# Front of a hybrid layer reordered: early modulation block, five weight buffers, moments of one tile first; GpSimd makes the filter parts' differences and VectorE their sums

## What is computed

```python
sh1, sc1, g1, sh2, sc2, g2 = split(silu(c) @ w_mod + b_mod, 6)   # once for c_ctx, once for c
u = layer_norm(x) * (1.0 + sc1) + sh1
q, k, v, xr, gate, hy = split(u @ w_in)
# hyena filters, for L = 128 and L = 512:
h = sin(freq[0] * (feats @ w1 + b1))
h = sin(freq[1] * (h @ w2 + b2))
h = (h @ w3).reshape(L, 4, 256) * exp(-t * abs(decay))
# forward and backward parts make one circular filter, used through its Fourier transform
filt_f = rfft(concat([f_fwd, 0, flip(f_bwd[:, 1:])]))
```

## Time and profile before

| what | value |
|---|---|
| median of three runs | 634.93 us (634.59, 634.93, 637.37) |
| the profiled execution's own time | 633.17 us |
| its span | 631.3 us |
| TensorE busy | 600.8 us, 95% |
| VectorE busy | 440.5 us, 70% |
| ScalarE busy | 305.6 us, 48% |
| GpSimd busy | 188.4 us, 30% |
| mean granted clock of TensorE | 0.997 |

### The profile page before, as it was taken

The page is one execution under the profiler, slowest core; times in us unless marked ns, Lnnn a source line. Parts: engine busy times, 40 slices in busy tenths (PEclk is TensorE's granted clock), DMA queues, the critical chain, the costliest instruction groups (busy, mean ns, idle before and its releaser), DMA issues.

```text
span 631.3 us, 9327 instructions
## 1 busy us (share of the span) xinstructions
PE 600.8 (95%) x3353; PEld 455.3 (72%) x3353; DVE 440.5 (70%) x757; ACT 305.6 (48%) x506; POOL 188.4 (30%) x152
## 2 busy tenths in 40 slices
PE   6899999999999988998999999989999999999994
PEld 2237999999999965557888888747767677676352
DVE  4967766834994654467553499988998877983187
ACT  2748122335344543005795342846565655752354
POOL 1002333345551307041496070421212221321121
PEclk9999999999999999999999999999999999999998
DMA  9985852222221269764980706769999999999788
GB/s 305 387 305 222 305 186 97 101 101 100 101 68 66 92 238 325 303 264 99 290 271 36 294 8 234 280 168 370 393 376 403 390 388 406 374 364 372 291 299 144
DMA packets 40040, 154.89 MB, mean 245 GB/s; under 512 B 7049, under 2 KB 17033, under 8 KB 27451
## 3 DMA queue, kind: packets, MB, share of 16 engines
q1 hardware_dynamic: 27912, 115.41, 50.6%
q10 hardware_dynamic: 5522, 23.48, 9.4%
q0 software_dynamic: 6560, 15.42, 8.3%
HBM read 141.59 MB, written 23.63 MB: 262 GB/s over the span
## 4 chain that ended last, share of the span: by engine, by line
PE 82%; DVE 7%; DMA 5%; ACT 4%; issue 2%; POOL 0%; DVEq 0%; ACTq 0%; POOLq 0%
PE bank L1898 13%; PE bank L1574 12%; PE bank L1575 12%; PE bank L1770 9%; PE bank L1952 8%; PE bank L1410 3%; PE bank L1747 2%; PE bank L1674 2%; PE bank L1880 2%; DMA arena<-in_w_mod 2%; PE bank L1477 2%; PE bank L1625 2%; PE bank L2011 2%; PE bank L1730 2%; DMA u_scr<-arena 1%
## 5 line engine op out<-in xcount | busy, mean ns | idle before, releaser
L772 POOL TENSOR_TENSOR w_low<-arena,w_high 128x1024 fp32r<-128x1024 f32 x22 | 53.6, 2437 | 145.9 <-ACT w_high L971 145.9
L2544 DVE TENSOR_TENSOR gate_up_low<-arena,gate_up_high 128x1024 fp32r<-128x1024 f32 x64 | 75.3, 1221 | 12.3 <-ACT gate_up_high L1256 10.2
L1256 ACT ACTIVATE gate_up_high<-arena 128x1024 fp32r<-128x1024 f32 x64 | 63.9, 1054 | 15.5 <-DMA arena<-in_moe_w_gu 15.5
L971 ACT ACTIVATE w_high<-arena 128x1024 fp32r<-128x1024 f32 x22 | 23.2, 1058 | 87.8 <-PE bank L1575 87.0
L1574 PE MATMUL bank<-u_high,w_high 128*128 128x320 f32 x176 | 56.3, 320 | 1.7 <-DVE u_low L2157 1.7
L1952 PE MATMUL bank<-arena 128*128 128x512 f32 x128 | 57.7, 593 | 0.0
L1575 PE MATMUL bank<-u_high,w_low 128*128 128x320 f32 x176 | 54.4, 309 | 0.0
L1574 PE MATMUL bank<-u_high,w_low 128*128 128x320 f32 x176 | 54.4, 309 | 0.0
L1574 PE MATMUL bank<-u_low,w_high 128*128 128x320 f32 x176 | 54.4, 309 | 0.0
L1575 PE MATMUL bank<-u_low,w_high 128*128 128x320 f32 x176 | 54.4, 309 | 0.0
L1575 PE MATMUL bank<-u_high,w_high 128*128 128x320 f32 x176 | 54.4, 309 | 0.0
(11 more groups left out here) (442 smaller groups left out, 1396.4 us busy)
## 6 DMA issues: line engine op xcount, KB each, us to landing
arena<-in_moe_w_gu SPq DMA_DIRECT2D x38, 1024.0 KB, 10.1
arena<-in_w_mod SPq DMA_DIRECT2D x24, 1024.0 KB, 6.6
arena<-in_moe_w_down ACTq DMA_DIRECT2D x13, 1024.0 KB
arena<-in_w_in SPq DMA_DIRECT2D x11, 1024.0 KB, 4.8
arena<-in_moe_w_down SPq DMA_DIRECT2D x6, 1024.0 KB
y_scr<-arena SPq DMA_DIRECT2D x11, 512.0 KB, 9.1
arena<-in_x SPq DMA_DIRECT2D x10, 512.0 KB, 9.6
arena<-y_scr SPq DMA_DIRECT2D x10, 512.0 KB, 6.0
```

The lines of the kernel that those rows point to most:

```text
L772: G.tensor_tensor(WL[s_][:, :, w], ring[s_][:, :, w], WH[m % 2].bitcast(F), ALU.subtract).then_inc(wl_rdy, 1)
L971: S.activation(WH[m % 2], ring[(m // 2) % 2][:, :, (m % 2) * P:(m % 2 + 1) * P], ACT.Copy).then_inc(wh_rdy, 1)
L1256: S.activation(WGH[j][c], raw_gu[s][:, c, :, :], ACT.Copy).then_inc(wgh_rdy, 1)
L2544: tt_(WGL[s][c], raw_gu[s][:, c, :, :], WGH[j][c].bitcast(F), ALU.subtract).then_inc(wgl_rdy, 1)
```

## The change

Five edits. The filter table is transferred as 33 rows of 704, and w2 as a table of its own. SyncE's queue brings modulation blocks 0 and 1 between the tiles of x, and the blocks use five buffers, two of them also those of W_in's first pieces. TensorE computes mod block 0 ahead of the filter rows and blocks 1 and 2 a place earlier than before, with fewer dense products, and spectrum(1, 1) ahead of mod block 7. VectorE takes the moments of one tile of x before the second fold instead of two, writes a filter tile's products over the windows, and makes only the sum; GpSimd makes the difference. At the end of the first projection piece, VectorE makes the last low parts of u ahead of a half of the last spectrum.

```diff
@@ filter table
-        filt = fl.take(NTOK + HIDDEN + P)
-        feats, w1, w2 = filt[:, 0:NTOK], filt[:, NTOK:NTOK + HIDDEN], filt[:, NTOK + HIDDEN:NTOK + HIDDEN + P]
+        filt = fl.take(NTOK + HIDDEN)
+        feats, w1 = filt[:, 0:NTOK], filt[:, NTOK:NTOK + HIDDEN]
+        w2 = fl.take(P)
...
+        mod1_in = mod_in + win_in
...
-        mod1_buf = [arena[:, MTAT:MTAT + 2048], arena[:, MTAT + 2048:MTAT + 4096], flat[1]]
+        mod1_buf = [arena[:, MTAT:MTAT + 2048], arena[:, MTAT + 2048:MTAT + 4096], flat[1], flat[2], flat[0]]
...
-            eng.wait_ge(win_in[p % 2], 16 * (p // 2 + 1))
+            eng.wait_ge(win_in[p % 2], 16 * (p // 2 + 2))
@@ SyncE's queue
-            for i in range(TT):
-                eng.dma_start(X[:, i, :], t["x"][i * P:(i + 1) * P, :]).then_inc(ld_x[i], 16)
...
-                if k >= 3:
-                    eng.wait_ge(mod1_mm, k - 2)
-                eng.dma_start(mod1_buf[k % 3], t["w_mod"][k * P:(k + 1) * P, 0:2048]).then_inc(mod_in[k % 3], 16)
+                if k >= 5:
+                    eng.wait_ge(mod1_mm, k - 4)
+                eng.dma_start(mod1_buf[k % 5], t["w_mod"][k * P:(k + 1) * P, 0:2048]).then_inc(mod1_in[k % 5], 16)
...
-                if p == 1:
-                    eng.wait_ge(mod1_mm, 6)
+                if p < 2:
+                    eng.wait_ge(mod1_mm, 8 if p else 5)
...
-            for k in range(KT):
+            def x_rows(i):
+                eng.dma_start(X[:, i, :], t["x"][i * P:(i + 1) * P, :]).then_inc(ld_x[i], 16)
+
+            for i in range(TT):
+                x_rows(i)
+                if i in (0, 2):
+                    mod1_block(i // 2)
+            for k in range(2, KT):
                 mod1_block(k)
@@ GpSimd, ahead of the low halves of W_in
+            for a in range(TT):
+                i = FILTER_ORDER[a]
+                eng.wait_ge(eo_win, a + 1)
+                G.tensor_tensor(OD[:, i, :], WN[:, i, 0:512], WN[:, i, 512:1024], ALU.subtract).then_inc(od_rdy, 1)
@@ ScalarE
-            eng.dma_start(filt, t["filt"]).then_inc(ld_filt, 16)
+            eng.dma_start(filt[0:FEATS, :], t["filt"]).then_inc(ld_filt, 16)
+            eng.dma_start(w2, t["hy_w2"]).then_inc(ld_filt, 16)
...
             eng.wait_ge(eo_rdy, TT)
+            eng.wait_ge(od_rdy, TT)
             for g in range(2):
                 S.activation(mrow1[g], mod_rows(B[4], g), ACT.Copy).then_inc(m1_ev, 1)
@@ TensorE, spectrum(g, odd)
+                if q:
+                    eng.wait_ge(od_rdy, 4 if odd else 2)
...
-            def front_dense(n):
+            def front_dense(n, bank=5):
...
             front_dense(1)
             filter_layer(0)
-            front_dense(4)
+            front_dense(3)
             filter_layer(1)
-            eng.wait_ge(modc_in, 1)
-            front_dense(4)
+            eng.wait_ge(cond_rdy, 2)
+            mod1(0)
+            front_dense(2)
             eng.wait_ge(filt_sin, 2)
             eng.wait_ge(ld_tables, 64)
             filter_rows([(0, 0), (1, 1)])
-            mod1(0)
+            mod1(1)
             eng.wait_ge(filt_read, 2)
             filter_rows([(2, 1), (4, 0)])
-            mod1(1)
+            mod1(2)
+            eng.wait_ge(eo_win, 1)
+            front_dense(1, 0)
             eng.wait_ge(eo_win, 2)
             filter_rows([(3, 1)], 2)
-            mod1(2)
             spectrum(0, 0)
...
             mod1(6)
+            spectrum(1, 1)
             mod1(7)
-            spectrum(1, 1)
@@ VectorE, filter_parts(a)
-                tt_(EV[:, i, :], b0[:, :], WN[:, i, 0:512], ALU.mult)
+                near, far = WN[:, i, 0:512], WN[:, i, 512:1024]
+                tt_(near, b0[:, :], near, ALU.mult)
                 if i < 2:
 
-                    stt(OD[:, i, :], b1[:, :], col("not0"), WN[:, i, 512:1024], ALU.mult, ALU.mult).then_inc(eo_win, 1)
+                    stt(far, b1[:, :], col("not0"), far, ALU.mult, ALU.mult).then_inc(eo_win, 1)
                 else:
-                    tt_(OD[:, i, :], b1[:, :], WN[:, i, 512:1024], ALU.mult).then_inc(eo_win, 1)
+                    tt_(far, b1[:, :], far, ALU.mult).then_inc(eo_win, 1)
                 after(eo_win)
-                step(tt_(EV[:, i, :], EV[:, i, :], OD[:, i, :], ALU.add))
-                if i < 2:
-                    eng.wait_ge(ld_tables, 64)
-                last = stt(OD[:, i, :], OD[:, i, :], -2.0, EV[:, i, :], ALU.mult, ALU.add)
+                last = tt_(EV[:, i, :], near, far, ALU.add)
                 if i < 2:
                     step(last)
+                    eng.wait_ge(ld_tables, 64)
                     last = tt_(EV[0:1, i, :], EV[0:1, i, :], skip[0:1, :], ALU.add)
@@ VectorE, the order
             filter_fold(0)
             x_moments(0)
-            x_moments(1)
             filter_fold(1)
-            for i in range(2, TT):
+            for i in range(1, TT):
                 last = x_moments(i)
...
             eng.wait_ge(mod1_mm, KT)
+            eng.wait_ge(od_rdy, TT)
             for g in range(2, 4):
...
-                if k == 7:
-                    spectrum_far(3)
             u_low(KT - 2)
+            spectrum_far(3)
+            u_low(KT - 1)
             spectrum_near(3)
-            u_low(KT - 1)
```

More of the change, by code:

```diff
@@ L478, in build @@
         scalar_st = sem("scalar_st")
-        modc_in = sem("modc_in")
+        od_rdy = sem("od_rdy")
         eo_win = sem("eo_win")
@@ L1413, in mod1 @@
             def mod1(k):
-                eng.wait_ge(mod_in[k % 3], 16 * (k // 3 + 1))
-                mod_block(B[4], k, mod1_buf[k % 3]).then_inc(mod1_mm, 1)
+                eng.wait_ge(mod1_in[k % 5], 16 * (k // 5 + 1))
+                mod_block(B[4], k, mod1_buf[k % 5]).then_inc(mod1_mm, 1)
             def filter_layer(layer):
@@ L1423, in filter_layer @@
                 else:
-                    eng.wait_ge(ld_filt, 16)
+                    eng.wait_ge(ld_filt, 32)
                     for half in range(2):
@@ L1486, in ctx_spectrum @@
                 mm(B[3][:, :], TAPSc[1], OD[:, 0, :], start=True, stop=True).then_inc(spec_mm, 1)
-            def front_dense(n):
+            def front_dense(n, bank=5):
                 for b in range(n):
-                    mm(B[5][:, :], ident, consts[:, 2 * KT:2 * KT + 512], start=True, stop=True)
+                    mm(B[bank][:, :], ident, consts[:, 2 * KT:2 * KT + 512], start=True, stop=True)
             front_dense(1)
             filter_layer(0)
-            front_dense(4)
+            front_dense(3)
             filter_layer(1)
-            eng.wait_ge(modc_in, 1)
-            front_dense(4)
+            eng.wait_ge(cond_rdy, 2)
+            mod1(0)
+            front_dense(2)
             eng.wait_ge(filt_sin, 2)
@@ L1593, in mod2 @@
             def mod2(b):
-                eng.wait_ge(mod_in[b % 3], 16 * ((3, 3, 2)[b % 3] + b // 3 + 1))
+                eng.wait_ge(mod_in[b % 3], 16 * (3 + b // 3))
                 mod_block(B[b // KT], b % KT, mod2_buf[b % 3]).then_inc(mod2_mm, 1)
@@ L2042, in _ @@
             step(stt(sig, sig, 1.0, cond, ALU.add, ALU.mult))
-            ts_(cond, sig, 0.5, None, ALU.mult).then_inc(modc_in, 1)
-            after(modc_in)
+            ts_(cond, sig, 0.5, None, ALU.mult).then_inc(cond_rdy, 1)
+            eng.wait_ge(cond_rdy, 2)
             magic = 1.5 * 2.0 ** 23
@@ L2909 @@
     pair2[0:HIDDEN, 0:HIDDEN] = pair2[HIDDEN:P, HIDDEN:P] = a["hy_w2"][0]
-    filt = np.zeros((P, NTOK + HIDDEN + P), f32)
-    filt[0:FEATS, 0:NTOK] = features()
-    filt[0:FEATS, NTOK:NTOK + HIDDEN] = a["hy_w1"][0]
-    filt[:, NTOK + HIDDEN:] = pair2
+    filt = np.concatenate([features(), a["hy_w1"][0]], 1).astype(f32)
     rgw = np.zeros((P, 8, P), f32)
@@ L2938 @@
         "brt": np.concatenate([a["router_bg"][0], a["router_be"][0]]),
-        "filt": filt, "hy_w3": a["hy_w3"][0],
+        "filt": filt, "hy_w2": pair2, "hy_w3": a["hy_w3"][0],
         "decay": a["hy_decay"][0].reshape(-1), "dft_taps": spec_tables, "dft": fold_tables,
```

## The result

| | before | after |
|---|---|---|
| median, us | 635.19 (633.47 to 637.37, 10 executions) | 641.85 (637.68 to 645.39, 10 executions) |
| the profiled execution's own time | 633.17 | 638.60 |
| its span, mean granted clock | 631.3, 0.997 | 636.4, 0.991 |

The ratio is 1.0097, 95% interval 1.0074 to 1.012: slower by 6.7 us where +2.5 was forecast, and the time lies above the range of 634.3 to 640.0. The ten executions after, with their mean granted clocks: 637.68 and 638.60 (0.991), 638.95 and 640.18 (0.990), 641.64 (0.989), 642.05 (0.986), 643.23 and 644.19 (0.983), 643.38 (0.981), 645.39 (0.982). The lower the clock, the longer the time, over 7.7 us; before spans 3.9 us.

A forecast was written before the change was run, and what follows sets the result against it. The prediction took TensorE to bound the kernel, with 82% of the chain that ended last. Its terms, +2.6 + 1.35 - 1.43, summed to +2.5 us, or 637.4 us on the median, with a range of 634.3 to 640.0.

The forecast's parts named there:

- moments 3 start, x3 landed: VectorE's moments of x tile 3, due at 19.84, wait for its later transfer and start at 21.3.
- filter parts start: VectorE's first filter tile starts at 24.2 instead of 22.15, +2.05, because x4 lands only at 22.65.
- skip addition blocked: VectorE's one-row skip addition of tile 1 waits for GpSimd's difference, both reading SBUF: +1.27, bounds 0 and 1.27.
- T0: When TensorE's last filter rows start: 27.04 before, forecast 29.66, about +2.6.
- T1 - T0: From last filter rows to little (m1) transposes on TensorE: 19.10 before, forecast 20.45, +1.35.
- tail: End of projection m = 0: low parts of u ahead of spectrum halves start its last slice 1.43 us earlier.
- front shift: Shift carried unchanged behind the first projection (m = 0): +2.6 + 1.35 - 1.43 = +2.5 us.
- rival D: TensorE's clock falls to the lower level after some 3 us idle in the front: +6.0, 640.9; chance 0.13.
- rival C: x3 and x4 land in time, filter parts at 22.74: +1.1, 636.0; chance 0.18, including the case with B.
- The first term: One dense product less before layer 2 on TensorE, so VectorE's second fold ends at 16.94 instead of 17.80: -0.86.
- rival B: The skip addition isn't blocked, VectorE gets in ahead of GpSimd: -1.27, so +1.2, 636.1; chance 0.14.
- T1: When the little (m1) transposes start on TensorE: 46.14 before, forecast +3.95.

The follow-up runs named there:

- b_tail: The kernel before with only the new order at the end of m = 0 (low parts of u ahead of spectrum halves): 633.57 us, ratio 0.9972.
- a_filled: The changed kernel with three more dense products ahead of tile 0's filter rows, filling TensorE's 3.26 us idle stretch: 638.54 us, ratio 1.0055.
- best: The change with x first, old mod block places, two tiles' moments ahead of the second fold, GpSimd behind the skip addition, new tail: 632.57 us, ratio 0.9947.
- a_mods_back: The changed kernel with modulation block 7 ahead of spectrum(1,1) again, as before had it: 636.56 us, ratio 1.003.
- a_skip_first: The changed kernel with GpSimd's differences waiting for the finished sum, so the skip addition goes before them: 640.11 us, ratio 1.0089.
- a_front_back: The changed kernel with x first on the queue and TensorE's blocks 0, 1 and 2 behind the filter rows as before: 638.50 us, ratio 1.0038.
- a_x_first: The changed kernel with all five tiles of x ahead of the modulation blocks on the queue, TensorE's order left as changed: 639.36 us, ratio 1.0089.
- b_gap: The kernel before with only modulation block 1 moved from ahead of the last filter rows to behind them: 638.54 us, ratio 1.0052.
- a_again: The changed kernel itself, unedited, in one more profiled execution: 644.77 us at a mean clock of 0.982.

## Why the prediction was wrong

| step | forecast | measured (profiled execution after) |
|---|---|---|
| moments 1 start, behind the second fold | 16.94 | 17.66 |
| moments 3 start, x3 landed | 21.3 | 22.09 |
| filter parts start | 24.2 | 25.05 |
| skip addition blocked | +1.27 | +0.95 (1.64 for 0.69) |
| VectorE releases T0 | 29.66 | 30.11 |
| T0 | 29.66 | 31.20 |
| T1 - T0 | 20.45 | 20.63 |
| tail | -1.43 | 5.69 - 4.27 = -1.42 |
| front shift | +2.5 | +4.27 |

**The step that failed** is that T0 is set by VectorE alone, with TensorE at full pace; the prediction had the fall of the clock only as rival D, at 0.13, and D's 640.9 is nearer the measured 641.85 than the forecast's 637.4. The idle stretch was foreseen in place and length (3 us up to 25.6; it was 3.26 up to 26.45), and so was the level. Two things were misjudged. The evidence against it, that the idle 1.37 left the clock up, was one execution: b_tail fell behind the same stretch. And D was priced as one fall of one length, behind T0; in the profile after it ended just ahead of T0, and the weight loads of T0's rows took 0.19 and not the 0.34 that was to decide it. What the runs showed is a draw: in one execution T0 came 1.1 us behind VectorE's release, in the other 2.2 (31.69 for 29.50), with 3.8 more lost behind T0 and 1.7 at a second stretch. That stretch, the uncovered copies ahead of T1, stood in the prediction's own working and was never held against the clock. The Trainium skill, page "TensorE: Matmul & The Clock Gate", section "Part 1: The HAM clock gate", says of the start of a kernel that the number of products at the low clock is "run-variable". Here it is the fall in the middle of the front that differed between two executions of one program (638.60 and 644.77).

**In the median**, after minus a_filled is 3.3 us, good to some 2: what the first idle stretch costs through the clock. Together with the forecast 2.5, the 0.45 that VectorE released T0 later and the 0.18 of T1 - T0 that is 6.4 of the 6.7 us, an estimate, since the first is from medians and the last two are from one execution. a_filled stands 3.3 over before, near the +2.5 of the terms. That it comes out so close is in part luck: before's own falls are in its median, and a_filled keeps the second idle stretch; no run sizes either.

**x** (rival C at 0.18) was decided against C: x was even later than I took it, by 0.8. I had given back 0.65 for the smaller filter table; x3 landed at 22.1 (3.9 + 18.2), which is the bound at which nothing is given back (half a block, 1.2, ahead of 23.3). The 21.3 itself should have been 22.65 - 1.2 = 21.45. This is one execution: in the five others of this queue order moments 3 started at 21.48 to 22.95, so x alone moves the front by up to 1.5 us between executions.

**The first term** (-0.86) was mis-sized: the moments behind the second fold started at 17.66 for 17.80 before, so only 0.14 came. With one dense product less, layer 2 met TensorE still at its starting pace: its two passes took 1.15 us for 0.81. The wait for x hid the difference. In best, with the same dense products ahead of it, they did start at 16.94, so this too differs between executions.

**The blocked addition** (rival B) was decided for the mechanism: 1.64 beside 0.68 when alone. Its size was 0.95 and not 1.27, as VectorE's sum went first and the subtraction was by that difference some 0.3 us on its way when the addition came. The Trainium skill, page "SBUF — State Buffer", section "Who interferes with whom", has this exclusion as a rule, and both traces agree (0.16 us became 2.31 before, 0.69 became 1.64 after). But undone alone it gave nothing, because TensorE, not VectorE, was last at T0 by then.

**T1** was right in the interval (20.63 for 20.45), and of the edits that were undone alone this is the dearest: moving one block back gives 2.6 us of T1 and 5.3 us of the median. The forecast saw +1.35 only because block 2's move ahead of T0 was set against it in the same sum.

**The tail** was right: -1.42 here, -1.5 in b_tail and best, for -1.43. The agreement to 0.01 us is luck.

**Left open**: what comes up between the front and the end. From the low half of the last piece to the end it was +0.8 here, +1.1 in best, +2.0 in a_filled and +3.4 in a_mods_back, against one profiled execution of before; b_tail had -0.1. Most of it comes up behind 350 us, in the mixture of experts. In the profile after a part of it is again the clock: from 420 to 424 us the granted clock is 0.57, behind small products with waits of 0.57 and 0.89 that before has too, and ten passes of a dense product take 6.23 us where before's took 4.54. a_skip_first has the same fall (0.60 there); a_mods_back has none, so its +3.4 is something else. Nor is it settled why a_front_back's median lies 4 us above its own quickest execution.

## What to carry to other kernels

Price an idle stretch of the matrix engine twice: for its own length, and for the slow work behind it, which differs from one execution to the next; a single profile at full clock doesn't show that it is safe. When work is moved ahead to fill a wait, look at what covered the wait that it left. Before a transfer is moved forward, list who now waits behind it, and undo both orders, the queue's and the engine's, when testing it.

## What the runs showed of the hardware

- In the front the clock fell behind idle stretches of 3.64, 3.26, 3.06, 2.39 and 2.37 us, inside one of 8.12, in one execution behind 1.69, and in two kernels behind 1.37. It did not fall in before's profile (1.37), in a_mods_back's (2.08), in best's (0.65), nor behind the 1.68 or 1.69 ahead of T1 in after, a_filled, a_skip_first, a_x_first and a_front_back. At 420 us it fell in two profiles, after and a_skip_first, behind waits of 0.57 and 0.89.
- From the granted clock by stretch, the lower level lasted some 3 us in most falls, some 7 in b_gap and a_x_first and 13.6 in a_again, there with TensorE busy all the time. Against the profile after, with its 3 us, T1 came 4.3 us later in a_again, though x was 0.6 earlier.
- At the lower level the filter rows took 3.78 us for 1.98, and a modulation block of 32-column products 1.93 for 1.06.
- The mean granted clock of an execution also counts its end: from 628 to 632 us of before it is 0.50, with no matrix product there. So it orders the executions only roughly.
- The granted clock reads 1.00 from 4 to 16 us in the profiles before and after, while weight loads took 0.34 and later 0.19 us. This row doesn't show the slow start; the durations do.
- The record of a GpSimd subtraction is longer where VectorE's sum went first: 1.77 us, and 1.27 where it didn't. It seems to contain the wait.
